# A decoder layer with product-key experts on one core: 160 instead of 144 gathered picks, dense products 352 columns wide

## Chip, core and metric

The kernel runs on one core of one Trainium2 chip. The metric is the time of one launch on the device in microseconds (us). Times of the kernel before are the median of three runs.

## What is computed

One layer for 512 tokens of width 2048, in float32. It has multi-head latent attention and a chunked spatial gating unit, an output projection, a PEER retrieval over 16,384 single-neuron experts, a gated per-layer embedding and a final norm. The change is about PEER alone:

```python
q = (a @ w_q).reshape(B, S, 8, 256)
s1, s2 = scores of the two halves of q against k1, k2      # 128 keys each, per head
...                                                        # top 16 of each, then top 16 of the 256 sums
experts = ...                                              # (token, head, 16): indices into 16,384 rows
gates = softmax(top)
h = einsum(u_exp[experts], a)                              # one dot product of 2048 per pick
out = einsum(gates * gelu(h), v_exp[experts])              # weighted sum of rows of v_exp
```

A token uses 8 x 16 = 128 of the 16,384 experts. `u_exp` and `v_exp` are 128 MB each.

## The kernel before

**Two ways to do PEER.** The tokens are split. The first `TD` = 368 tokens go the dense way: every expert is computed for every one of them. The weights of `u_exp` pass through as 128 chunks of 1 MB (128 experts each); a chunk gives a product of 128 experts by 368 tokens, which is scaled (`scale_chunk`, L1369), passed through gelu on ScalarE (L766) and stored to memory (`pre`). The gates of the dense tokens are scattered by GpSimd with indirect adds (`add_gates`, L518, 384 of them, one for each of three token tiles, 8 heads and 16 picks) into a matrix in memory that is zero but for the picks (`gates`, blanked by the fills of L488). Later each chunk of pre-activations and gates is loaded (L404, L405), multiplied on GpSimd (`apply_gates`, L545), split in a high and a low part (ScalarE L822, `weight_lo` L1475) and multiplied with `v_exp`, which passes as 16 groups of 8 slots of 1 MB. The result is added to the residual `hT` (`accumulate`, L1480).

The other 144 tokens go the sparse way: rows are gathered. A gather fetches one row of `uv_rows` (u and v side by side, 16 KB) for each of 128 partitions, 2 MB, by an indirect DMA that GpSimd issues (`gather`, L537). VectorE forms the dot products with the u half (`dot`, L1449), ScalarE makes gelu times gate of them (`weigh_pick`, L839 and L843), and VectorE adds the weighted v half to an accumulator (`add_row`, L1458, L1463). Two kinds of picks exist. *A picks* (`A_PICKS` = 128): the last 128 tokens, one token on each partition, one pick each. *B picks* (`B_PICKS` = 16): `BT` = 16 further tokens, each on 8 partitions (`SETS` = 8), one for each head, so 16 gathers cover their 128 picks. Their index tables are rearranged by small DMAs on ScalarE's queue (`bring_set`), their activations are spread by `spread_tokens`, and at the end a matmul with `sel` sums the partitions of a token.

**Matmuls.** Weights and activations are split in two float32r parts, and each product is three matmuls (`three`, L1637 to L1639: high x high, high x low, low x high). The high part of a weight tile is a copy by ScalarE (`hi`, L582), the low part a subtraction by VectorE (`lo`, L967), both for each MB of the stream. `wH` and `wL` have two buffers. The raw tiles have two, and four in most of the V stage (`raw_at`).

**Order.** Every engine's program is in order and written out by hand. In the head stage each of 8 heads takes two tiles of the query projection (512 columns) and four U chunks, with the top-k search on VectorE. Then come U chunks 32 to 127. From chunk 36 on the steps of the picks are spread over the slots: a pick has two steps, the dot and the add, and `u_step(c)` and `v_step(g, q)` say how many half steps are done before a slot. Picks 0 to 59 lie in the chunks up to 118, four more in the last eight chunks, and the rest, up to `PICKS` = 144, in the 118 V slots from the third to the end of group 14. The last group has none. A VectorE slot of V is: accumulate, first pick step, `lo`, other pick steps, accumulate, `weight_lo`. The row tiles: three buffers for the first picks, then two in turn (`ROW_AT`). A gather waits until the pick that used its buffer is added (`pick_done`). GpSimd does 164 scatter-adds (`ADDS_FIRST`), then gathers with four adds between them until the 384 are done, then `apply_gates` with the later gathers between. SyncE issues the raw loads, and in V between each two of them one chunk of pre-activations and gates (`load_late_chunk`), which waits for `act_wlo` of the chunk before the last.

Of the kernel before, what the change touches and what calls it, by code (L numbers as in the profile page):

```python
# [27 lines left out]
HEADS = 8  # L28
# [4 lines left out]
TOPK = 16  # L33
KEYS = 128
EPS = 1e-6
BT = 16
TA = T - P
TD = TA - BT
NTD = NT - 1
SETS = P // BT  # L40
PARTS = SETS // HEADS
A_PICKS = HEADS * TOPK
B_PICKS = TOPK // PARTS
PICKS = A_PICKS + B_PICKS
GROUP = 8
NGROUPS = KEYS // GROUP
# [105 lines left out]
def trunk_layer(nc, a, stream, out, gates_dram, pre_dram):  # L152
    F, R, U32, I32 = mybir.dt.float32, mybir.dt.float32r, mybir.dt.uint32, mybir.dt.int32
# [5 lines left out]
    KB = 1024  # L159

    def at(name, shape, dt, offset):
        return nc.alloc_sbuf_tensor_at(name, [P] + shape, dt, offset=base + offset)


    H0, A0, RING0, W0, M0, C0 = 0, 32 * KB, 96 * KB, 144 * KB, 176 * KB, 192 * KB
# [80 lines left out]
    ident = at("ident", [P], F, C0 + 12 * KB)  # L246
    iota = at("iota", [TOPK], F, C0 + 12 * KB + 512)
    idx_b = at("idx_b", [B_PICKS], U32, C0 + 12 * KB + 576)
    gates_b = at("gates_b", [B_PICKS], F, C0 + 12 * KB + 640)
    dots_b = at("dots_b", [B_PICKS], F, C0 + 12 * KB + 704)  # L250
    pick_wb = at("pick_wb", [B_PICKS], F, C0 + 12 * KB + 768)
    sel = at("sel", [BT], F, C0 + 12 * KB + 832)
    identR = at("identR", [P], R, C0 + 13 * KB)
    causalR = at("causalR", [P], R, C0 + 13 * KB + 512)
    dots = at("dots", [P], F, C0 + 13 * KB)
    pick_w = at("pick_w", [P], F, C0 + 13 * KB + 512)
    ones = at("ones", [P], F, C0 + 14 * KB)
    gains = at("gains", [NGAINS], F, C0 + 14 * KB + 512)
    smax = at("smax", [32], F, C0 + 14 * KB + 864)
# [10 lines left out]
    with ctx:  # L270
# [298 lines left out]
        def _(act):  # L569
# [136 lines left out]
            for n in range(ITEMS + 3):  # L706
# [16 lines left out]
                if n >= 5 and (n - 5) % NT == 3:  # L723
                    h = (n - 5) // NT
# [121 lines left out]

            def bring_set(i):

                h, r = divmod(i, PARTS)
                dst = slice(i * BT, (i + 1) * BT)  # L850
                src = slice(h * TOPK + r * B_PICKS, h * TOPK + (r + 1) * B_PICKS)
                act.dma_start(idx_b[dst, :], idx_e[at_b:P, src]).then_inc(b_loaded, 16)
                act.dma_start(gates_b[dst, :], gates_r[at_b:P, NTD - 1, src]).then_inc(b_loaded, 16)

            for c in range(ROUTE_U + 2, KEYS - GROUP):
                u_beat(c, c % 2, nu + c, 0)
                if c == ROUTE_U + 6:
                    act.wait_ge(routed, HEADS)
                if 0 <= c - ROUTE_U - 6 < SETS:
                    bring_set(c - ROUTE_U - 6)  # L860
                for o in range(u_step(c), u_step(c + 1)):
                    if o % 2 == 0:
                        weigh_pick(o // 2)
# [91 lines left out]
        def _(dve):  # L955
# [415 lines left out]
            def spread_tokens():  # L1371

                r4 = b_rep[:, :, :].rearrange("p k (r t) -> p k r t", t=BT)
                st.did(V.tensor_tensor(r4, hT[:, :, TD:TA].unsqueeze(2).to_broadcast([P, KD, SETS, BT]),
                                       gains[:, GAINS["ffn"]:GAINS["ffn"] + KD].unsqueeze(2).unsqueeze(3)
# [711 lines left out]
```

## Time and profile before

| | |
|---|---|
| median of 3 runs | 3095.76 us (3092.18 to 3096.97) |
| the profiled execution, its own time | 3098.32 us |
| its span, first to last instruction | 3096.6 us |
| mean granted TensorE clock | 0.994 |
| busy: TensorE, VectorE, ScalarE, GpSimd | 98%, 72%, 34%, 39% |
| memory traffic | 768.6 MB, mean 248 GB/s |

The page gives busy times by engine, the span in 40 slices of 77 us (busy tenths, granted clock, GB/s), the chain of work that ended last, and groups of instructions. A matmul's duration reaches from its start to the end of its pipeline and overlaps the next; the distance of two starts is what it takes of TensorE's time. The DMA share is the mean busy share of the core's 16 DMA engines; over short windows it can exceed 1.

### The profile page before, as it was taken

Reading aid. Unit: us, or ns where it says so; the run is one execution under the profiler, and the core shown is the slowest. Engines: PE = TensorE matmul, PEld = TensorE weight load, DVE = VectorE, ACT = ScalarE, POOL = GpSimd, SP = SyncE. Lnnn points to the kernel's source line nnn. Section 1 sums busy time; section 2 is a strip of 40 time slices with the busy share of each in tenths; the row PEclk is TensorE's granted clock in tenths of the full one; section 3 lists DMA queues with packets and bytes.
Section 4 is the critical chain, followed back from the end, with each engine's and each line's share of the span. In section 5 each row is a group of like instructions: output and inputs, shape, how many; then the busy total and the mean of one; then the engine's idle time right before and its main releaser. Section 6 shows DMA issues by size and latency. Waiting matters only on the chain.

```text
span 3096.6 us, 42534 instructions
## 1 busy us (share of the span) xinstructions
PE 3043.2 (98%) x16860; PEld 2854.9 (92%) x16860; DVE 2226.1 (72%) x2944; ACT 1061.3 (34%) x1328; POOL 1206.3 (39%) x702
## 2 busy tenths in 40 slices
PE   8999999999999999999999999999999999998998
PEld 6888668899999999999999999999999999998887
DVE  5465653478778777777777658888888888985545
ACT  5224442333332433333333333333333333333422
POOL 1010000018888788788887112332332333440000
PEclk9999999999999999999999999999999999999999
DMA  8472212245545599999999779899989989873222
GB/s 305 145 248 85 106 51 98 83 130 129 131 125 131 136 362 352 342 350 350 340 332 366 276 313 352 347 358 362 360 354 364 356 339 370 352 302 135 100 95 95
DMA packets 191488, 768.59 MB, mean 248 GB/s; under 512 B 68609, under 2 KB 121873, under 8 KB 129393
## 3 DMA queue, kind: packets, MB, share of 16 engines
q1 hardware_dynamic: 90768, 407.45, 35.9%
q0 software_dynamic: 81632, 335.12, 30.2%
q10 hardware_dynamic: 18944, 24.14, 2.3%
q8 instruction: 85, 1.39, 0.2%
q14 instruction: 59, 0.48, 0.0%
HBM read 714.00 MB, written 52.62 MB: 248 GB/s over the span
## 4 chain that ended last, share of the span: by engine, by line
PE 92%; DVE 3%; DMA 2%; issue 1%; ACT 1%; SPq 0%; POOL 0%; POOLq 0%; DVEq 0%; ACTq 0%
PE ps L1637 30%; PE ps L1638 30%; PE ps L1639 30%; DMA gate_in<-gates 1%; DVE wL L967 1%; DMA raw<-s_pu 1%; PE ps L1810 1%; PE ps L1829 1%; PE ps L1809 1%; PE ps L1872 0%; DMA raw<-s_v 0%; ACT wH L582 0%; DVE hT L1458 0%; DVE ssum L979 0%; PE ps L1819 0%
## 5 line engine op out<-in xcount | busy, mean ns | idle before, releaser
L1637 PE MATMUL ps<-aH,wH 128*128 128x368 f32 (+2 forms) x3088 | 1075.5, 348 | 6.5 <-DVE wL L967 4.4
L1638 PE MATMUL ps<-aL,wH 128*128 128x368 f32 (+2 forms) x3088 | 1071.6, 347 | 0.0
L1639 PE MATMUL ps<-aH,wL 128*128 128x368 f32 (+2 forms) x3088 | 1071.6, 347 | 0.0
L582 ACT ACTIVATE wH<-raw 128x2048 fp32r<-128x2048 f32 x333 | 637.7, 1915 | 1015.3 <-PE ps L1639 881.2
L967 DVE TENSOR_TENSOR wL<-raw,wH 128x2048 fp32r<-128x2048 f32 x333 | 786.2, 2361 | 195.3 <-ACT wH L582 194.4
L518 POOL DMA_INDIRECT gates<-gates_r,idx_d x384 | 745.9, 1942 | 370.5 <-DVE gates_r L1360 237.5
L1637 PE MATMUL ps<-actH,wH 128*128 128x368 f32 x2048 | 676.4, 330 | 12.5 <-DVE wL L967 10.3
L1638 PE MATMUL ps<-actL,wH 128*128 128x368 f32 x2048 | 675.7, 330 | 0.0
L1639 PE MATMUL ps<-actH,wL 128*128 128x368 f32 x2048 | 675.4, 330 | 0.0
L1637 PEld LDWEIGHTS ps<-aH,wH 128*128 128x128 f32 x3088 | 580.2, 188 | 46.4 <-DVE wL L967 5.5
L1638 PEld LDWEIGHTS ps<-aL,wH 128*128 128x128 f32 x3088 | 580.3, 188 | 38.7 <-issue 1.0
L1639 PEld LDWEIGHTS ps<-aH,wL 128*128 128x128 f32 x3088 | 580.2, 188 | 38.5
L1637 PEld LDWEIGHTS ps<-actH,wH 128*128 128x128 f32 x2048 | 386.4, 189 | 13.8 <-DVE wL L967 11.3
L1638 PEld LDWEIGHTS ps<-actL,wH 128*128 128x128 f32 x2048 | 386.4, 189 | 0.0
L1639 PEld LDWEIGHTS ps<-actH,wL 128*128 128x128 f32 x2048 | 386.4, 189 | 0.0
L545 POOL TENSOR_TENSOR pre_in<-pre_in,gate_in 128x368 f32<-128x368 f32 x128 | 181.4, 1417 | 434.1 <-DMA gate_in<-gates 431.8
L537 POOL DMA_INDIRECT rows<-uv_rows,idx_s x128 | 214.6, 1676 | 333.8 <-DVE hT L1458 295.9
L1449 DVE SCALAR_TENSOR_TENSOR rows<-rows,ps 128x2048 f32<-128x2048 f32 x128 | 291.6, 2278 | 16.3 <-DMA rows<-uv_rows,idx_s 15.8
L1458 DVE SCALAR_TENSOR_TENSOR hT<-rows,pick_w,hT 128x2048 f32<-128x2048 f32 x128 | 300.3, 2346 | 0.0
L1369 DVE TENSOR_TENSOR ut<-ps,rstd 128x368 f32<-128x368 f32 x128 | 69.1, 540 | 211.0 <-PE ps L1639 191.9
L1480 DVE TENSOR_TENSOR hT<-hT,ps 128x368 f32<-128x368 f32 x256 | 135.7, 531 | 93.5 <-PE ps L1639 93.5
L1475 DVE TENSOR_TENSOR actL<-pre_in,actH 128x368 fp32r<-128x368 f32 x128 | 85.6, 669 | 50.7 <-ACT actH L822 50.7
(258 smaller groups left out, 1890.5 us busy)
## 6 DMA issues: line engine op xcount, KB each, us to landing
raw<-s_pu SPq DMA_DIRECT2D x128, 1024.0 KB
raw<-s_pv SPq DMA_DIRECT2D x128, 1024.0 KB
gates<-zeros POOLq DMA_DIRECT2D x23, 1024.0 KB, 8.5
pre<-ut ACTq DMA_DIRECT2D x128, 184.0 KB
pre_in<-pre SPq DMA_DIRECT2D x128, 184.0 KB
gate_in<-gates SPq DMA_DIRECT2D x128, 184.0 KB
raw<-s_out SPq DMA_DIRECT2D x16, 1024.0 KB
raw<-s_pq SPq DMA_DIRECT2D x16, 1024.0 KB
```

Of the source, the lines that this page charges most:

```text
L518: pool.indirect_dma_start(out=gates_flat, out_offset=bass.IndirectOffsetOnAxis(ap=idx_d[0:m, t, c:c + 1], axis=0), in_=gates_r[0:m, t, c:c ...
L537: pool.indirect_dma_start(out=rows[ROW_AT[j]][:, :, :].rearrange("p a d -> p (a d)"), out_offset=None, in_=a["uv_rows"], in_offset=bass.In ...
L545: nc.gpsimd.tensor_tensor(pre_in[b][:, :], pre_in[b][:, :], gate_in[b][:, :], ALU.mult).then_inc(act_gated, 1)
L582: A(wH[parity][:, :], raw[at_n][:, :], ACT.Copy).then_inc(hi_ready, 1)
L967: V.tensor_tensor(wL[parity][:, :], src[:, :], wH[parity][:, :].bitcast(F), ALU.subtract).then_inc(lo_ready, 1)
L1449: V.scalar_tensor_tensor(r3, r3, 1.0, act_of, ALU.mult, ALU.mult, accum_out=d).then_inc(dot_done, 1)
L1458: V.scalar_tensor_tensor(hT[:, :, TA:T], v3, pick_w[:, j:j + 1], hT[:, :, TA:T], ALU.mult, ALU.add).then_inc(pick_done, 1)
L1475: V.tensor_tensor(actL[b][:, j, 0:TD], src[:, :], actH[b][:, j, 0:TD].bitcast(F), ALU.subtract).then_inc(act_wlo, 1)
L1480: V.tensor_tensor(h, h, ps[:, 4 + k % 4, 0:TD], ALU.add).then_inc(h_acc, 1)
L1637: mm(out, wh, xh, start=start, stop=False)
L1638: mm(out, wh, xl, start=False, stop=False)
L1639: return mm(out, wl, xh, start=False, stop=stop)
```

## The change

The split of the tokens moves by 16. `BT` becomes 32, so `TD` becomes 352 and every dense product, store, load, multiplication and accumulate has 352 columns. The b tokens are 32, each on 4 partitions (`SETS` = 4); a partition takes the picks of a pair of heads, 32 (`B_PICKS`), so the picks are 160. `v_step` spreads 96 instead of 80 of them over the same 118 V slots; `u_step` does not depend on their number. The gates' fills become 22. The small tables of the b picks are moved: `dots_b` and `pick_wb` are now views of the first columns of `dots` and `pick_w`, the tables of the A picks.

```diff
-BT = 16
+BT = 32
 TA = T - P
 TD = TA - BT
 NTD = NT - 1
 SETS = P // BT
-PARTS = SETS // HEADS
 A_PICKS = HEADS * TOPK
-B_PICKS = TOPK // PARTS
+B_PICKS = A_PICKS // SETS
 PICKS = A_PICKS + B_PICKS
...
-    gates_b = at("gates_b", [B_PICKS], F, C0 + 12 * KB + 640)
-    dots_b = at("dots_b", [B_PICKS], F, C0 + 12 * KB + 704)
-    pick_wb = at("pick_wb", [B_PICKS], F, C0 + 12 * KB + 768)
+    gates_b = at("gates_b", [B_PICKS], F, C0 + 12 * KB + 704)
...
+    dots_b, pick_wb = dots[:, 0:B_PICKS], pick_w[:, 0:B_PICKS]
...
-                h, r = divmod(i, PARTS)
                 dst = slice(i * BT, (i + 1) * BT)
-                src = slice(h * TOPK + r * B_PICKS, h * TOPK + (r + 1) * B_PICKS)
+                src = slice(i * B_PICKS, (i + 1) * B_PICKS)
```

## Rows read from the trace of the kernel before

**Rows 1.** The page: GB/s in the 40 slices of 77 us.
```profile
GB/s 305 145 248 85 106 51 98 83 130 129 131 125 131 136 362 352 342 350 350 340 332 366 276 313 352 347 358 362 360 354 364 356 339 370 352 302 135 100 95 95
```
**Rows 2.** The page: the chain that ended last, share of the span by line.
```profile
PE ps L1637 30%; PE ps L1638 30%; PE ps L1639 30%; DMA gate_in<-gates 1%; DVE wL L967 1%; DMA raw<-s_pu 1%; PE ps L1810 1%; PE ps L1829 1%; PE ps L1809 1%; PE ps L1872 0%; DMA raw<-s_v 0%; ACT wH L582 0%; DVE hT L1458 0%; DVE ssum L979 0%; PE ps L1819 0%
```
**Rows 3.** TensorE's waits, the longest in total: us, times, longest us.
```profile
PE ps L1637 <- DVE wL L967: 15.8, 7, 6.1
```
**Rows 4.** Stretches: length, busy us of PE, PEld, DVE, ACT, POOL; clock, DMA share, GB/s.
```profile
1100.00:1700.00 600.00, 600.00 (x3602) 600.00 (x3601) 451.55 (x316) 201.36 (x262) 482.87 (x268) 1.00 0.97 347
...
1762.00:1861.00 99.00, 95.46 (x572) 94.86 (x571) 62.48 (x52) 35.98 (x43) 14.78 (x15) 1.00 0.77 299
...
1900.00:2700.00 800.00, 800.00 (x4802) 800.00 (x4801) 697.37 (x604) 266.49 (x337) 268.37 (x168) 1.00 0.91 357
...
2770.00:2810.00 40.00, 30.27 (x166) 29.35 (x164) 21.67 (x18) 8.04 (x11) 3.89 (x4) 0.91 0.44 160
...
2064.00:2072.00 8.00, 8.00 (x50) 8.00 (x49) 6.56 (x8) 2.82 (x4) 1.66 (x2) 1.00 1.02 418
```
**Rows 5.** Timeline of TensorE: start us, duration us, neighbouring matmuls of 368 and of 512 columns.
```profile
860.15 0.33 PE L1639 MATMUL ps<-aH,wL 128*128 128x368 f32 x1
860.32 0.33 PE L1637 MATMUL ps<-aH,wH 128*128 128x368 f32 x1
...
2990.06 0.39 PE L1639 MATMUL ps<-aH,wL 128*128 128x512 f32 x1
2990.29 0.39 PE L1637 MATMUL ps<-aH,wH 128*128 128x512 f32 x1
```
**Rows 6.** Timeline of ScalarE in V: two weight copies, each released by TensorE.
```profile
2066.23 1.92 ACT L582 ACTIVATE wH<-raw 128x2048 fp32r<-128x2048 f32 x1 [5.68 <-PE ps L1639]
...
2074.23 1.92 ACT L582 ACTIVATE wH<-raw 128x2048 fp32r<-128x2048 f32 x1 [4.35 <-PE ps L1639]
```
**Rows 7.** Groups of VectorE by form: count, busy us, mean ns, idle before and releaser.
```profile
L967 DVE TENSOR_TENSOR wL<-raw,wH 128x2048 fp32r<-128x2048 f32 x333 | 786.2, 2361 | 195.3 <-ACT wH L582 194.4
L1458 DVE SCALAR_TENSOR_TENSOR hT<-rows,pick_w,hT 128x2048 f32<-128x2048 f32 x128 | 300.3, 2346 | 0.0
L1449 DVE SCALAR_TENSOR_TENSOR rows<-rows,ps 128x2048 f32<-128x2048 f32 x128 | 291.6, 2278 | 16.3 <-DMA rows<-uv_rows,idx_s 15.8 <-issue 0.2
L1480 DVE TENSOR_TENSOR hT<-hT,ps 128x368 f32<-128x368 f32 x256 | 135.7, 531 | 93.5 <-PE ps L1639 93.5
```
**Rows 8.** V, 1900 to 2700 us: two gathers, dots that waited for them, all such waits.
```profile
2160.17 0.96 POOL L537 DMA_INDIRECT rows<-uv_rows,idx_s  x1 [0.16 <-issue]
...
2549.97 2.85 POOL L537 DMA_INDIRECT rows<-uv_rows,idx_s  x1 [0.16 <-issue]
...
2171.29 2.29 DVE L1449 SCALAR_TENSOR_TENSOR rows<-rows,ps 128x2048 f32<-128x2048 f32 x1 [0.56 <-DMA rows<-uv_rows,idx_s]
...
2563.61 2.29 DVE L1449 SCALAR_TENSOR_TENSOR rows<-rows,ps 128x2048 f32<-128x2048 f32 x1 [0.90 <-DMA rows<-uv_rows,idx_s]
...
DVE rows L1449 <- DMA rows<-uv_rows,idx_s: 9.6, 11, 1.6
```
**Rows 9.** U: gathers, two of the dots, and the gathers' waits for a free buffer.
```profile
1077.96 1.00 POOL L537 DMA_INDIRECT rows<-uv_rows,idx_s  x1 [3.77 <-DVE ps L1435]
...
1089.97 1.00 POOL L537 DMA_INDIRECT rows<-uv_rows,idx_s  x1 [0.30 <-issue]
...
1614.60 1.36 POOL L537 DMA_INDIRECT rows<-uv_rows,idx_s  x1 [0.30 <-issue]
...
1684.70 1.00 POOL L537 DMA_INDIRECT rows<-uv_rows,idx_s  x1 [0.30 <-issue]
...
1090.54 2.27 DVE L1449 SCALAR_TENSOR_TENSOR rows<-rows,ps 128x2048 f32<-128x2048 f32 x1
...
1626.54 2.27 DVE L1449 SCALAR_TENSOR_TENSOR rows<-rows,ps 128x2048 f32<-128x2048 f32 x1
...
POOL rows L537 <- DVE hT L1458: 17.9, 11, 3.0
```

## The prediction

> **What bounds the kernel now.** I read the page first. TensorE is busy for 98% of the span (the table above), and the core's memory traffic jumps from about 130 to about 350 GB/s a third of the way in, where the row gathers begin [rows 1]. The chain that ended last is nine tenths TensorE, three lines with 30% each, the dense products [rows 2]. The list of TensorE's waits then shows how little it ever stands still: the largest entry is 15.8 us in 7 waits, for the low half of a weight tile [rows 3]. So a matmul that gets shorter is paid out in full, as long as all that feeds TensorE keeps up. The stretches [rows 4] say how near the feeders are to their own limits. In 600 us of the U stage TensorE never rests, VectorE is busy for 452 us (0.75), GpSimd for 483, and the DMA engines 0.97, moving 347 GB/s. In 800 us of the V stage TensorE never rests either, VectorE is busy for 697 us (0.87) and the DMA engines 0.91, moving 357 GB/s. That is the reader's main point: TensorE is the bound, but two or three others stand within a tenth behind it, and this change shortens TensorE's work and lengthens theirs.
>
> **The matmuls.** Neighbouring matmuls of 368 columns start 166 to 167 ns apart, those of 512 columns 227 ns [rows 5]. The difference, 60 ns for 144 columns, is 0.42 ns a column; so 352 columns should take 160 ns. A chunk of U (16 blocks times 3) or a slot of V (2 tiles times 8 times 3) has 48 of them: 8.00 us now, which is what two starts of the weight copy show [rows 6], and 7.68 us after. There are 256 such units: 256 x 0.32 = 82 us if TensorE stays the bound everywhere. The granted clock is 1.00 (the 2.4 GHz level) in all long dense stretches [rows 4].
>
> **The head stage, 32 chunks of U.** Up to 1046 us traffic is about 130 GB/s [rows 1] and no picks run. Nothing else is near its limit: 32 x 0.32 = **-10.2 us**.
>
> **U chunks 32 to 119, 88 of them, picks 0 to 59.** At best -28.2 us. The picks' number does not change here (60 over 82 chunks), their pace does: one in 10.93 us before, one in 10.49 after. Two things can hold this back. GpSimd: gather 2 starts at 1089.97 and gather 56 at 1684.70, 11.01 us each, of which it waited only 17.9 us in all for a free buffer [rows 9]; its own pace, with four scatter-adds between gathers, is (594.7 - 17.9) / 54 = 10.7 us, a little slower than 10.49. The lead of a gather over its dot product falls to 11.9 us at its tightest (1614.60 to 1626.54), about a landing time [rows 8, 9]. And the first gather: the 164 adds ahead of it do not get quicker, so it starts at best 3.8 us earlier (it had waited that long), while the chunks stand 10.2 us earlier; the 12.6 us between it and its dot (1077.96 to 1090.54) become about 6 [rows 9], and VectorE waits some 5 us once. The DMA engines: a chunk moves 1.05 MB of weights, 0.18 of stores and 0.73 x 2.10 of rows, 2.76 MB; at 7.68 us that is 360 GB/s, where 347 took a share of 0.97, so 358 a full one [rows 4]. I take 10 us as given back (between 0 and 20): **-18 us**.
>
> **The changeover, chunks 120 to 127 and the first V slots.** TensorE is busy only 95.5 of 99 us, VectorE 62.5 and the DMA engines 0.77 [rows 4]: nobody is full, so what is awaited there are loads and buffers in turn, not work. A faster TensorE waits longer: **0** (bounds -5 and +5). The same for the five slots at 2770 to 2810, busy 30.3 of 40 us at clock 0.91: **0**. The last eight V slots, without picks: **-2.6 us**.
>
> **V slots with picks, some 106 beside those.** Picks 64 to 159 instead of 64 to 143 go into the same 118 slots: 0.814 a slot instead of 0.678. TensorE alone would give 106 x -0.32 = -34 us. Against it stand three prices.
> - VectorE: a pick costs 2.28 + 2.35 = 4.63 us [rows 7]. At 0.136 more per slot that adds 0.63 us to the 6.97 us of now (697 us in 100 slots) [rows 4]; columns fewer give back some 0.06 (2.35 us for 2048 columns is 1.15 ns a column; three operations with 16 fewer). 7.54 us of 7.68: all but full, not over.
> - DMA: a slot moves 1.05 (weights) + 0.36 (gates and pre-activations) + 0.814 x 2.10 (rows) = 3.12 MB instead of 2.85. At 7.68 us that is 406 GB/s. The V row gives 357 GB/s at 0.91, so 392 at a full share: 7.95 us. One window of 8 us did show 418 GB/s [rows 4], so the edge is not hard.
> - Row tiles: two buffers in turn, so dot product, weight split and row add (2.3 + 2.4 + 2.35 = 7.0 us), then the gather, must fit into two picks, 2.46 slots. Gathers that VectorE waited for took 11.1 us (2160.17 to 2171.29) and 13.6 us (2549.97 to 2563.61) from GpSimd's start [rows 8]. With 0.2 us to start a gather that makes (7.2 + 11.1) / 2.46 = 7.4 us (no bound) and (7.2 + 13.6) / 2.46 = 8.46 us a slot.
>
> The prices meet in one in-order VectorE, whose lateness reaches the weight split and so TensorE. I take 8.10 us, above the DMA edge of 7.95 and below 8.46: 106 x 0.10 = **+11 us**.
>
> The Trainium skill, "DMA: Bandwidth & Descriptors", section "Where 436 GB/s comes from", puts the fabric's ceiling at 435 GB/s and says that transfers from HBM are bound at about 358 GB/s per core. By the first the slot would be 3.12 / 435 = 7.2 us, an estimate, and by the second 8.7 us. The window at 418 GB/s speaks for the first; the plateau of 339 to 370, 356 in the mean, in eleven slices of the V stage [rows 1] looks like the second.
>
> **Small edits.** 22 instead of 23 blank fills, and 8 instead of 16 small loads of indices and gates on ScalarE's queue: both lie behind TensorE's uninterrupted work of their stages, and without that cover they would be a gain, not a loss: 0. The sum of the b tokens is 512 instead of 256 wide; by the accumulate of 368 columns in 0.53 us [rows 7] that is some 0.3 us more on VectorE, in the last V slots, where it has room: 0. No wait is added for a chunk or a slot, but behind a late row on VectorE now stand the next weight split, the accumulates and the activation split, and SyncE's next loads wait for those.
>
> **Sum.** -10.2 - 18 + 0 - 2.6 + 11 = -20 us against the profiled execution's own 3098.3 us (span 3096.6): 3078. That execution stood 2.6 us above the median of 3095.8, so 3075.5 as a median. Differences of under 0.2% (6 us) can't be told from none here.
>
> **Rivals.**
> 1. *TensorE stays the bound* because the DMA engines reach 406 GB/s, as they did 418 for 8 us. V slots at 7.75: 106 x -0.25 = -26.5, U in full -28.2, with the rest -67: 3028. Against it: 0.91 x 3.12 / 2.85 x 8 / 7.68 = 1.04 of a full share. 0.16.
> 2. *The two row tiles decide* (slower). Place: the gather of pick j+2 behind the add of pick j. Price: 8.46 us a slot if every landing takes the 13.6 us of the longer one, 106 x 0.46 = +49, -31 elsewhere: +18, 3113. It decides once a landing takes over 2.46 x 8.00 - 7.2 = 12.5 us. For it: the longer landing is above that already, and landings should lengthen as the DMA engines fill. Against it: the other is below, and only 11 of some 68 dots (0.678 a slot) waited for a row at all, 9.6 us in sum [rows 8]. 0.19.
> 3. *The memory rate does not rise above its plateau*, say 360 GB/s: 3.12 / 360 = 8.67 us a slot, 106 x 0.67 = +71, with the rest +40: 3136. The 8 us window at 418 speaks against it. The figure of 358 GB/s per core in the Trainium skill ("DMA: Bandwidth & Descriptors", section "Where 436 GB/s comes from") would be this case. 0.08.
>
> **The forecast's own range**: slots from 7.95 (-5) to 8.25 us (+26), U between -28 and -8: 3047 to 3101; chance 0.57. The range 3032 to 3120 takes in rival 2 and half of rival 1, and leaves out rival 3 and the tails. Faster: nine tenths of the forecast and rival 1, 0.66; same 0.08; slower 0.26.
>
> **What would show it.** Matmul starts 160 ns apart; heads 1.28 us shorter; in the V stretches DMA share 0.97 or more near 385 GB/s, VectorE over 0.93 busy, TensorE waiting for the weight split for the first time in mid-stretch, some 0.4 us a slot; dots waiting for rows in most slots. Wrong: V stretches with TensorE still at 1.00 (rival 1), or a granted clock below 1.00 there after long waits, which no row prices for this stretch and which would push towards rival 2 or beyond.

## The result: 0.35% slower, and the profile after

Before: 3098.0 us, the median of twelve runs (3092.2 to 3105.2). After: 3108.3 us, the median of twelve runs on the same chip (3099.4 to 3125.2). The ratio is 1.0035, with a 95% interval of 1.0023 to 1.0046. The forecast was a gain of 20 us; the change costs 10.

Three lines of the changed kernel's page: the granted clock and the GB/s in the 40 slices (78 us each), and the chain that ended last, by line [rows 1, 2].

```profile
PEclk9999999999999999999999999999999999998999
GB/s 302 148 234 86 105 55 95 88 126 139 121 137 133 183 359 345 352 369 354 349 352 362 278 353 368 399 366 386 378 367 365 396 357 368 371 310 136 102 95 95
...
POOL gates L516 22%; PE ps L1634 10%; PE ps L1635 10%; PE ps L1636 10%; DMA rows<-uv_rows,idx_s 8%; DMA gate_in<-gates 6%; DMA rows<-uv_rows,idx_b 4%; DVE wL L964 4%; DVE hT L1455 3%; DVE rows L1446 3%; POOL rows L535 2%; DVE b_acc L1460 1%; DMA gates<-gates_r,idx_d 1%; DVE hT L1477 1%; POOL pre_in L543 1%
```

The chain was nine tenths TensorE before. Now a third of it is TensorE, and 12% is the landing of gathered rows, which was no part of it. (The 22% of L516 are the scatter-adds of the U stage. TensorE rests for only 2 of 600 us there, so the chain probably had two nearly equal ways back; the positions below show that this stage did get faster.)

The stretches: length, busy us of PE, PEld, DVE, ACT, POOL, then clock, DMA share and GB/s [rows 4].

```profile
1100.00:1700.00 600.00, 597.94 (x3710) 597.36 (x3709) 467.03 (x327) 206.09 (x270) 480.48 (x266) 1.00 1.00 357
...
1762.00:1861.00 99.00, 91.12 (x552) 89.67 (x551) 67.87 (x60) 34.18 (x41) 21.08 (x18) 0.98 0.87 343
...
1900.00:2700.00 800.00, 760.86 (x4620) 752.48 (x4619) 712.17 (x617) 258.75 (x349) 276.58 (x174) 0.98 0.95 374
...
2770.00:2810.00 40.00, 29.26 (x166) 28.09 (x164) 25.65 (x23) 8.29 (x12) 5.65 (x4) 0.91 0.56 212
```

In the 800 us of the V stage TensorE now stands still for 39 us. Neither of the two feeders that I had at their edge is there: VectorE is busy for 712 us (0.89) and the DMA share is 0.95. The waits of that stretch, for TensorE and for VectorE, name what is late:

```profile
PE ps L1634 <- DVE wL L964: 38.9, 25, 4.2
...
DVE rows L1446 <- DMA rows<-uv_rows,idx_s: 43.0, 28, 4.5
DVE actL L1472 <- ACT actH L820: 16.6, 30, 0.6
DVE hT L1477 <- PE ps L1636: 15.7, 18, 1.9
DVE rows L1446 <- DMA rows<-uv_rows,idx_b: 12.1, 11, 2.9
```

The kernel before, same stretch:

```profile
DVE hT L1480 <- PE ps L1639: 74.6, 55, 2.2
```

VectorE waits 55 us for gathered rows (10 before, [rows 8]) and little for TensorE (15.7 us; it was 74.6). All of TensorE's idle time comes from the weight split behind such a row. Here is one case from the timeline, VectorE's dot products (L1446), row adds (L1455), splits (L964), GpSimd's multiplication (L543) and gathers (L535), and the matmul that waited:

```profile
2261.03 2.34 DVE L1455 SCALAR_TENSOR_TENSOR hT<-rows,pick_w,hT 128x2048 f32<-128x2048 f32 x1
...
2264.16 2.22 POOL L543 TENSOR_TENSOR pre_in<-pre_in,gate_in 128x352 f32<-128x352 f32 x1 [7.34 <-DMA gate_in<-gates]
2265.50 2.28 DVE L1446 SCALAR_TENSOR_TENSOR rows<-rows,ps 128x2048 f32<-128x2048 f32 x1
2266.53 0.97 POOL L535 DMA_INDIRECT rows<-uv_rows,idx_s  x1
...
2271.91 2.28 DVE L964 TENSOR_TENSOR wL<-raw,wH 128x2048 fp32r<-128x2048 f32 x1
2272.26 2.78 POOL L535 DMA_INDIRECT rows<-uv_rows,idx_s  x1 [3.40 <-DVE hT L1455]
...
2278.64 2.29 DVE L1446 SCALAR_TENSOR_TENSOR rows<-rows,ps 128x2048 f32<-128x2048 f32 x1 [4.46 <-DMA rows<-uv_rows,idx_s]
2282.80 2.34 DVE L1455 SCALAR_TENSOR_TENSOR hT<-rows,pick_w,hT 128x2048 f32<-128x2048 f32 x1
2285.06 2.28 DVE L964 TENSOR_TENSOR wL<-raw,wH 128x2048 fp32r<-128x2048 f32 x1
2287.40 0.43 PE L1634 MATMUL ps<-actH,wH 128*128 128x352 f32 x1 [4.21 <-DVE wL L964]
```

The add that frees the row tile ends at 2263.37. GpSimd is held by a multiplication, which itself had waited for its gates, and starts the gather at 2266.53. The row is there 12.1 us later, at 2278.64. VectorE has stood for 4.46 us, and TensorE then for 4.21. The granted clock falls with it: it is 0.91 in the 10 us of this wait and 0.92 in the next 10.

```profile
2280.00:2290.00 10.00, 5.79 (x31) 5.50 (x31) 9.45 (x11) 4.87 (x6) 4.66 (x3) 0.91 0.66 242
2290.00:2300.00 10.00, 10.00 (x60) 10.00 (x59) 10.00 (x8) 2.81 (x4) 1.93 (x2) 0.92 1.03 424
2300.00:2310.00 10.00, 10.00 (x64) 10.00 (x63) 8.95 (x10) 3.49 (x7) 2.26 (x2) 1.00 1.01 407
```

**Where the time went, by position.** The table gives the start in us of the scaling of U chunks 31 and 127, of `weight_lo` of V slots 6, 110 and 119, and of the last two accumulates, in each profile. "A slot" is the distance of slots 6 and 110 over 104; "rows" is what dot products of the V stage waited for gathers. Each row is one execution. Kernels with the same U stage differ by up to 10 us at U 127, so a single difference means little under that size there, and under 5 us elsewhere. The variants are described in the next section.

| kernel | U 31 | U 127 | V 6 | V 110 | V 119 | last | a slot | rows |
|---|---|---|---|---|---|---|---|---|
| before | 1056.3 | 1830.2 | 1888.6 | 2720.3 | 2810.1 | 2881.3 | 8.00 | 10.5 |
| after | 1045.7 | 1798.4 | 1859.5 | 2726.0 | 2817.3 | 2889.0 | 8.33 | 63.6 |
| columns only | 1048.8 | 1808.5 | 1865.0 | 2668.3 | 2755.8 | 2825.5 | 7.72 | 25.2 |
| picks only | 1057.0 | 1831.3 | 1892.5 | 2761.8 | 2854.7 | 2924.9 | 8.36 | 63.4 |
| after, u half only | 1044.1 | 1801.1 | 1856.3 | 2663.8 | 2750.8 | 2820.6 | 7.76 | 0 |
| after, split rows | 1048.6 | 1809.0 | 1870.0 | 2695.4 | 2785.2 | 2855.0 | 7.94 | 0 |
| after, third tile | 1044.7 | 1804.3 | 1865.3 | 2695.6 | 2767.8 | 2837.7 | 7.98 | 0 |
| after, ring of two | 1047.3 | 1803.9 | 1859.8 | 2723.3 | 2801.4 | 2872.2 | 8.30 | 69.8 |
| before, ring of two | 1060.1 | 1834.3 | 1888.7 | 2720.4 | 2794.7 | 2866.6 | 8.00 | 7.7 |
| before, third tile | 1060.6 | 1834.3 | 1893.3 | 2725.2 | 2798.7 | 2873.0 | 8.00 | 0 |
| before, split rows | 1055.4 | 1829.5 | 1888.8 | 2720.8 | 2810.0 | 2881.1 | 8.00 | 0 |
| picks only, split rows | 1057.6 | 1831.7 | 1893.9 | 2750.6 | 2841.2 | 2911.5 | 8.24 | 0 |
| picks only, third tile | 1055.5 | 1830.2 | 1890.8 | 2727.9 | 2802.3 | 2874.6 | 8.05 | 0 |
| after, split rows, 160 adds | 1045.8 | 1798.6 | 1859.7 | 2685.6 | 2775.5 | 2845.4 | 7.94 | 0 |

After is 31.8 us ahead at the end of U and 29.1 at V slot 6. At slot 110 it is 5.7 behind. The 104 slots between lost 34.8 us.

### The profile page after: what moved, and what is told of

It reads as the page before. It is cut to its first block, busy times and chain, and to the rows that moved or that the text cites. A ratio compares the mean times of both kernels' runs of the same rounds, so it can differ in the third digit from the quotient of the medians.

```text
span 3104.3 us, 42637 instructions
## 1 busy us (share of the span) xinstructions
PE 2996.5 (97%) x16860; PEld 2795.3 (90%) x16860; DVE 2279.2 (73%) x2992; ACT 1062.5 (34%) x1360; POOL 1222.0 (39%) x717
## 4 chain that ended last, share of the span: by engine, by line
PE 32%; POOL 24%; DMA 19%; DVE 13%; issue 8%; ACT 2%; SPq 0%; POOLq 0%; ACTq 0%; DVEq 0%
POOL gates L516 22%; PE ps L1634 10%; PE ps L1635 10%; PE ps L1636 10%; DMA rows<-uv_rows,idx_s 8%; DMA gate_in<-gates 6%; DMA rows<-uv_rows,idx_b 4%; DVE wL L964 4%; DVE hT L1455 3%; DVE rows L1446 3%; POOL rows L535 2%; DVE b_acc L1460 1%; DMA gates<-gates_r,idx_d 1%; DVE hT L1477 1%; POOL pre_in L543 1%
## 5 line engine op out<-in xcount | busy, mean ns | idle before, releaser
L1634 PE MATMUL ps<-aH,wH 128*128 128x352 f32 (+2 forms) x3088 | 1063.9, 345 | 8.8 <-DVE wL L964 6.7
L1635 PE MATMUL ps<-aL,wH 128*128 128x352 f32 (+2 forms) x3088 | 1062.1, 344 | 0.0
L1636 PE MATMUL ps<-aH,wL 128*128 128x352 f32 (+2 forms) x3088 | 1059.6, 343 | 0.0
L964 DVE TENSOR_TENSOR wL<-raw,wH 128x2048 fp32r<-128x2048 f32 x333 | 780.5, 2344 | 196.0 <-ACT wH L580 193.4
L516 POOL DMA_INDIRECT gates<-gates_r,idx_d x384 | 758.9, 1976 | 370.3 <-DVE gates_r L1357 235.8
L1634 PE MATMUL ps<-actH,wH 128*128 128x352 f32 x2048 | 675.1, 330 | 63.3 <-DVE wL L964 60.3
L1635 PE MATMUL ps<-actL,wH 128*128 128x352 f32 x2048 | 670.2, 327 | 0.0
L1636 PE MATMUL ps<-actH,wL 128*128 128x352 f32 x2048 | 669.8, 327 | 0.0
L1446 DVE SCALAR_TENSOR_TENSOR rows<-rows,ps 128x2048 f32<-128x2048 f32 x128 | 292.1, 2282 | 70.3 <-DMA rows<-uv_rows,idx_s 69.2
L535 POOL DMA_INDIRECT rows<-uv_rows,idx_s x128 | 193.5, 1512 | 347.8 <-DVE hT L1455 312.3
L543 POOL TENSOR_TENSOR pre_in<-pre_in,gate_in 128x352 f32<-128x352 f32 x128 | 174.5, 1364 | 353.7 <-DMA gate_in<-gates 352.9
L1455 DVE SCALAR_TENSOR_TENSOR hT<-rows,pick_w,hT 128x2048 f32<-128x2048 f32 x128 | 300.6, 2349 | 0.4 <-ACT pick_w L841 0.3
L837 ACT ACTIVATE dots<-dots 128x1 f32<-128x1 f32 x160 | 32.5, 203 | 581.9 <-DVE rows L1446 540.4
L1366 DVE TENSOR_TENSOR ut<-ps,rstd 128x352 f32<-128x352 f32 x128 | 66.9, 523 | 165.7 <-PE ps L1636 117.6
L1477 DVE TENSOR_TENSOR hT<-hT,ps 128x352 f32<-128x352 f32 x256 | 130.8, 512 | 25.9 <-PE ps L1636 25.9
```

The lines of the kernel that those rows point to most:

```text
L516: pool.indirect_dma_start(out=gates_flat, out_offset=bass.IndirectOffsetOnAxis(ap=idx_d[0:m, t, c:c + 1], axis=0), in_=gates_r[0:m, t, c:c ...
L535: pool.indirect_dma_start(out=rows[ROW_AT[j]][:, :, :].rearrange("p a d -> p (a d)"), out_offset=None, in_=a["uv_rows"], in_offset=bass.In ...
L543: nc.gpsimd.tensor_tensor(pre_in[b][:, :], pre_in[b][:, :], gate_in[b][:, :], ALU.mult).then_inc(act_gated, 1)
L964: V.tensor_tensor(wL[parity][:, :], src[:, :], wH[parity][:, :].bitcast(F), ALU.subtract).then_inc(lo_ready, 1)
L1366: V.tensor_tensor(ut[b][:, :], ps[:, 6 + b, 0:TD], rstd[:, 0:TD], ALU.mult).then_inc(chunk_scaled, 1)
L1446: V.scalar_tensor_tensor(r3, r3, 1.0, act_of, ALU.mult, ALU.mult, accum_out=d).then_inc(dot_done, 1)
```

## The experiments

The main theory: the cycle of one of two whole row tiles (dot, split, add, gather, landing) is longer than two picks now last, and everything behind the late row is late. The rivals: VectorE is simply full; the memory rate is at its limit; and later, that the order of the raw loads holds the stage back. Each ratio is against the kernel before, run beside the variant on the same chip. The chips differ from group to group (the kernel before took 3095.4 to 3099.7 us on them), so medians of different groups compare to within some 4 us.

**Split rows.** One row tile is released in halves: the u half can be refilled once the dot has read it, the v half once the add has. The bytes, the picks and the matmuls stay.

```diff
-                        if o % 2 == 1 and o // 2 + 2 < PICKS:
-                            gather(o // 2 + 2)
+                        if o // 2 + 2 < PICKS:
+                            gather_half(o // 2 + 2, o % 2 == 1)
...
+                if ROW_USED[j] >= 0:
+                    pool.wait_ge(pick_done if out else dot_done, ROW_USED[j] + 1)
...
+                    out=rows[ROW_AT[j]][:, 1 if out else 0, :], out_offset=None, in_=a["v_rows" if out else "u_rows"],
```

> The changed kernel, but for picks 64 to 159 a row is fetched by two gathers, the u half and the v half, each into its half of the same two row tiles. The u half may be refilled after the dot product, the v half after the add. The same bytes; 96 more gather instructions on GpSimd. Theory A (the two row tiles decide: dot, weight split, add and a landing of 11 to 14 us must fit into two picks): each half has only 2.3 us of use in its cycle, so the V slot falls from 8.33 us to the DMA edge, 3.12 MB at a full share (374 GB/s at 0.95, so 394 GB/s), 7.92 us; 104 x 0.41 = 43 us less than the changed kernel, some 3065 us, and the waits of dots for rows shrink from 64 us to under 15. Theory B (the DMA engines' rate decides, about 374 GB/s over the V stage whatever the buffers do): slot 8.3 us, 3108 us as the changed kernel, GB/s unchanged. Theory C (VectorE's work decides): slot unchanged or longer by the slower instructions beside more gathers.

Measured: 3065.8 us (3061.3 to 3072.5), ratio 0.989 (0.9872 to 0.9908). The V stretch:

```profile
1900.00:2700.00 800.00, 782.72 (x4842) 776.49 (x4842) 772.41 (x651) 273.43 (x366) 471.61 (x266) 1.00 0.99 394
```

No dot of this stretch waits for a row any more, and the traffic flows at 394 GB/s instead of 374. GpSimd pays with 195 us more (one more indirect DMA a pick), which nothing waits for. The same picks and bytes pass faster, at a higher memory rate and with VectorE busier. So neither of these two had made the changed kernel slow.

**Columns only, picks only.** The change has two parts. The first kernel keeps the 352 columns and takes 144 picks, so half of the experts of the 32 b tokens are left out; the second keeps 368 columns and takes 160, 16 of them experts that the b tokens should not have.

```diff
-B_PICKS = A_PICKS // SETS
+B_PICKS = A_PICKS // SETS // 2
```
```diff
-B_PICKS = TOPK // PARTS
+B_PICKS = 2 * TOPK // PARTS
```

> The changed kernel with 144 picks: 352 columns in all dense products, but the 32 b tokens get only the first of their two heads on each partition (16 of 32 b picks are left out), so the output of those tokens lacks half of their experts. Shows what the narrower products give without more picks. Every theory: U as in the changed kernel (32 us less than before), V demand 2.83 MB a slot, 369 GB/s at 7.68 us, a share of 0.94, and two picks last 22.7 us against 7.2 + 13.6. Theory A: V slots 7.7 to 7.8 us, total 3098 - 32 - 104 x 0.25 = about 3040 us. Theory B (rate capped near 374): 7.68 us is 369, the same 3035 to 3045. If slots stay at 8.0, something not counted (GpSimd or the chunk loads) holds V.

> The kernel before with 160 picks: 368 columns and 16 b tokens as before, but each partition takes 32 b picks instead of 16, the additional 16 being those of the next head (for the last head those of the one before), so the b tokens sum too many experts. Shows what 16 more picks cost without narrower products. Theory A: slot max(8.0, (7.2 + landing) / 2.46) with landings of 11 to 14 us, 8.4 us or more: 104 x 0.4 = 42 us over before, 3140 us. Theory B: 3.14 MB at 374 GB/s is 8.4 us as well, and at 394 GB/s 8.0 us, 3098 to 3140. Theory C (VectorE, 7.6 us of work in an 8.0 us slot): no change, 3098 us.

Measured: columns 3040.9 us (3037.7 to 3045.1), ratio 0.9814 (0.9795 to 0.9834); picks 3141.0 us (3138.6 to 3145.6), ratio 1.0139 (1.0119 to 1.0158). The parts make 0.9814 x 1.0139 = 0.9950 together, the change 1.0035: they do more harm together than one by one, by 0.8% (26 us). The V stretches of both:

```profile
1900.00:2700.00 800.00, 798.82 (x4969) 797.30 (x4969) 702.06 (x624) 272.89 (x346) 266.20 (x173) 1.00 0.94 366
```
```profile
1900.00:2700.00 800.00, 775.95 (x4591) 769.92 (x4590) 716.49 (x617) 257.59 (x348) 266.00 (x174) 0.99 0.96 376
```

In the V slots the columns alone pay nearly in full (7.72 us, where TensorE needs 7.68), with a pick period of 11.4 us. The picks alone raise the slot to 8.36 us, what it is after (8.33), although each slot has 0.32 us more of matmuls: at 160 picks and two tiles the slot goes by the tiles and not by TensorE.

**The u half only.** The gathers of the V stage fetch 1 MB instead of 2, into the same tile with the same releases, and the add reads the u half. VectorE's work is unchanged.

```diff
+                half = ROW_AT[j] >= 3
...
-                    out=rows[ROW_AT[j]][:, :, :].rearrange("p a d -> p (a d)"), out_offset=None, in_=a["uv_rows"],
+                    out=rows[ROW_AT[j]][:, 0, :] if half else rows[ROW_AT[j]][:, :, :].rearrange("p a d -> p (a d)"), out_offset=None,
+                    in_=a["u_rows"] if half else a["uv_rows"],
```

> The changed kernel, but the gathers of picks 64 to 159 fetch only the u half of a row (1 MB instead of 2 for 128 partitions), and the add uses that half: VectorE's, GpSimd's and TensorE's instructions are the same, the gathered bytes of V are halved (v rows are left out of those picks). Theories A and B both: landings of 6 to 8 us and 2.27 MB a slot, 295 GB/s, so V slots reach TensorE's 7.68 us, 3098 - 32 - 104 x 0.32 = about 3033 us. Theory C (VectorE's 7.5 us of work, in order): slots of 8.0 us or more, 3065 us or more.

Measured: 3041.6 us, ratio 0.9817 (0.9792 to 0.9842).

```profile
1900.00:2700.00 800.00, 797.60 (x4948) 794.37 (x4947) 772.21 (x664) 275.02 (x371) 289.23 (x187) 1.00 0.81 292
```

VectorE is busy for 772 of 800 us (0.97), TensorE rests 2.4 us and a slot takes 7.76 us: a VectorE as full as that costs at most 0.08 us a slot. With shorter landings the two tiles are enough. This alone can't tell tiles from memory rate, since both landing and traffic fell; the split rows and the third tile do.

**Controls with split rows.** The split in the kernel before, in the kernel with 160 picks and 368 columns, and the split kernel with 160 scatter-adds ahead of the first gather instead of 164 (its first dot had waited 9.9 us).

> The kernel before (368 columns, 144 picks) with the split gathers of e1_split_rows. Theory A (row tiles decide only where 160 picks meet 7.68 us): here TensorE's 8.00 us was the bound and the tiles were just fast enough, so nothing is gained: 3093 to 3099 us, slot 8.00; dots no longer wait for rows. If the split were a gain by itself (fewer late weight splits, a clock that never falls), it would be over 6 us faster.

> e3_picks_only (368 columns, 160 picks, some experts of the b tokens summed twice over) with the split gathers. e3 cost 44.6 us over before. Theory A: the slot is the larger of TensorE's 8.00 us and the DMA edge, 3.13 MB at 394 GB/s, 7.95 us; so nearly all 44.6 us vanish, 3096 to 3108 us. Theory B (16 more picks cost DMA rate whatever the tiles do) or C (VectorE): 3125 us or more.

> e1_split_rows with 160 instead of 164 scatter-adds ahead of the first gather (one more gather later has four behind it). In e1 the first dot waited 9.9 us for its row (gather at 1083.2, dot at 1091.7), in the changed kernel 1.4 us. GpSimd's four adds are 7.4 us: the first gather starts that much earlier, but not before a_tok, which was ready at 1069.7. Expected 5 to 7 us less than e1: 3059 to 3061 us. If only GpSimd's total work counts in U, no change: 3066 us.

Measured: 3098.1 us, ratio 1.0003 (0.9992 to 1.0014); 3122.6 us (3119.0 to 3128.7), ratio 1.0071 (1.0052 to 1.009); 3065.4 us (3062.9 to 3070.1), ratio 0.9895 (0.9877 to 0.9914). The first is the control that was wanted: where rows are not late, the split gives nothing. The second is a miss: 18.5 us better than without the split, but some 15 to 27 us above what I expected, with slots of 8.24 us and no dot waiting. The third is a null in the medians, where I had expected 5 us or more. Its profile says otherwise: the first dot waited 1.5 us instead of 9.9, and the way from U 31 to U 127 took 752.8 us instead of 760.4. But that execution was the fastest of its kernel and the other the slowest of its own, so the two profiles don't overrule the medians, and the point stays open. The first dots of the split kernel and of the changed kernel:

```profile
1091.68 2.29 DVE L1462 SCALAR_TENSOR_TENSOR rows<-rows,ps 128x2048 f32<-128x2048 f32 x1 [9.92 <-DMA rows<-uv_rows,idx_s]
...
1080.35 2.29 DVE L1446 SCALAR_TENSOR_TENSOR rows<-rows,ps 128x2048 f32<-128x2048 f32 x1 [1.43 <-DMA rows<-uv_rows,idx_s]
```

**A third row tile.** Three whole tiles instead of two. The room comes from the raw ring, which stays at two buffers in V; SyncE then loads one chunk and one value in turn.

```diff
-    _at = _j % 3 if _j < U_PICKS - LATE else 2 if _j < U_PICKS else 3 + _j % 2
+    _at = _j % 3 if _j < U_PICKS - LATE else 2 if _j < U_PICKS else 3 + _j % 3
...
-    v = n - S0["pv"]
-    return (v - 2) % 4 if 4 <= v < KEYS - GROUP else n % 2
+    return n % 2
...
-            for v in range(2, KEYS - GROUP):
+            for v in range(KEYS - GROUP):
                 load_late_chunk(v)
-                load_value(v + 4)
+                load_value(v + 2)
...
-                        if o % 2 == 1 and o // 2 + 2 < PICKS:
-                            gather(o // 2 + 2)
+                        if o % 2 == 1 and o // 2 + 3 < PICKS:
+                            gather(o // 2 + 3)
```

> The changed kernel with whole-row gathers, but three row tiles in turn in V instead of two, gathers issued three picks ahead; the 16 KB for the third are taken from the raw ring, which has two tiles in V instead of four, with SyncE's loads reordered to chunk v, value v+2. Theory A: with three tiles a landing may take 3 x 2.46 / 2 slots = 28.3 - 8.0 = 20 us before it matters, so rows are never waited for; slot 7.95 us (DMA edge) if two raw tiles are enough, 3066 us. With raw loads of about 10 us (as the 10.4 us of the changeover) against some 9 us of slack, weight copies may wait for raw: then up to 8.2 us a slot and 3090 us, with ScalarE's L580-copy waiting for DMA raw instead of dots for rows. Theory B: 8.3 us a slot, 3108 us.

Measured: **3053.1 us** (3046.1 to 3057.0), ratio 0.9845 (0.9822 to 0.9868), the fastest version that computes the whole layer.

```profile
1900.00:2700.00 800.00, 780.86 (x4812) 771.36 (x4811) 762.02 (x645) 270.99 (x362) 293.50 (x182) 1.00 0.99 391
...
DVE actL L1466 <- ACT actH L814: 23.7, 38, 0.9
DVE wL L958 <- ACT wH L574: 14.1, 14, 2.2
```

No wait for rows is left, and VectorE (0.95) and the DMA engines (0.99) both stand near their edge: this is close to the state that I had forecast for the change itself, at 7.98 us a slot. The time is 13 us below the 3066 that I had expected. Slots 110 to 119 took 72.3 us instead of the 89.8 with split rows (91.4 after), so the kernel had two changes in it.

**The ring alone, and all combinations.** The ring of two and its load order without the third tile, in both kernels; the third tile with 160 picks and 368 columns; and the third tile in the kernel before.

> The kernel before (368 columns, 144 picks, two whole row tiles) with the raw ring and the load order of e8_third_tile: two raw tiles all through V, SyncE issues chunk v, then value v+2. In the kernel before, SyncE has a gap of 24 us in its raw loads (2751.2 to 2775.2) where the ring goes from four tiles to two, and TensorE idles 10 us behind it. Theory A takes the 12 us that e8 is faster than e1 for this gap alone (from slot 110 to 119 it took 72 us, e1 90): expected 10 to 17 us less than before, 3080 to 3087 us, with slots of 8.00 us elsewhere. If two raw tiles are too few at 8.00 us, slots grow and it is slower than before.

> The changed kernel with that ring and load order, but still two whole row tiles in V. Theory A (the row tiles): V slots from 6 to 110 stay at 8.3 us, only the end is 10 to 17 us shorter: 3091 to 3098 us, 40 us over e8. If the order of SyncE's loads was what the row tiles seemed to be (theory D: chunks come earlier when they don't queue behind a load four slots ahead), slots fall to 8.0 us and the time to 3055 us.

> e3_picks_only (368 columns, 160 picks, some experts of the b tokens summed twice) with ring, order and third row tile of e8. e6 (split gathers) left 25 us of e3's 45: slots of 8.24 us although no dot waited, TensorE waiting 1.4 us for a weight split every 42 or 90 us. If that rest is the unevenness of VectorE's in-order program (two slots in a row with two pick steps take 9.8 us each), it stays here too: slots of 8.1 to 8.2 us, and with the 10 to 17 us of the end 3098 to 3112 us. If it was the slower VectorE instructions beside 96 more gather instructions, slots are 8.0 us: 3085 us.

> The kernel before (144 picks, 368 columns) with a ring of two raw tiles, the load order of one chunk and one value in turn, and three whole row tiles in the V stage. It closes the table of picks against row tiles. Theory: at 144 picks two row tiles are no bound (the pick period is 11.8 us, and a late row cost the kernel with the ring of two and two tiles 7.7 us in all), so a third tile gives nothing: 3078 to 3084, the 3081.9 of that kernel, slot 8.00 us. Rival: a third tile helps any kernel (fewer late rows, or the gathers spread over time): under 3075, and then the 27 us between 3053 with 160 picks and 352 columns and 3082 are not all the change's.

| median us (ratio, 95%) | two row tiles, ring of four | two row tiles, ring of two | three row tiles, ring of two |
|---|---|---|---|
| 144 picks, 368 columns | 3098.0 | 3081.9 (0.9918 to 0.9962) | 3085.8 (0.9939 to 0.9973) |
| 160 picks, 368 columns | 3141.0 (1.0119 to 1.0158) | | 3094.6 (0.998 to 1.0001) |
| 160 picks, 352 columns | 3108.3 (1.0023 to 1.0046) | 3089.9 (0.9959 to 0.9991) | 3053.1 (0.9822 to 0.9868) |

Three things stand in it. The ring of two with its load order is worth 16 to 18 us by the medians in either kernel with two row tiles, most of it between slots 110 and 119 (15.5 us of the kernel before, 13.3 of the changed one). The window at slots 110 to 114 of the kernel before with the ring of two, against 30.27 busy us in [rows 4], is

```profile
2770.00:2810.00 40.00, 40.00 (x248) 39.98 (x246) 30.90 (x25) 13.73 (x16) 8.87 (x4) 1.00 0.66 237
```

The third tile is worth nothing at 144 picks (+4 us, intervals that overlap) and 37 us at 160 picks and 352 columns. And the change itself, from the first line to the last, costs 10 us with two tiles (8 with the ring of two) and gains 33 with three. The two V stretches side by side, with the ring of two in both (kernel after with two tiles, then kernel before with three):

```profile
1900.00:2700.00 800.00, 759.70 (x4627) 750.13 (x4626) 714.13 (x620) 259.08 (x349) 269.37 (x176) 0.99 0.95 376
```
```profile
1900.00:2700.00 800.00, 800.00 (x4802) 800.00 (x4801) 702.74 (x605) 266.70 (x336) 273.53 (x168) 1.00 0.90 357
```

The middle row bears on the miss above. With 160 picks and 368 columns the third tile gives slots of 8.05 us, nearly the 8.00 of TensorE, and the split rows only 8.24 (third tile, then split rows):

```profile
1900.00:2700.00 800.00, 797.70 (x4779) 795.89 (x4778) 760.57 (x640) 270.90 (x362) 290.80 (x181) 1.00 0.99 389
```
```profile
1900.00:2700.00 800.00, 783.44 (x4677) 778.59 (x4676) 750.82 (x625) 261.54 (x352) 442.26 (x256) 1.00 0.97 381
```

So most of what held the split kernel was not an unevenness of 160 picks as such. The two kernels differ in the split, which has one more gather a pick, and in the raw ring; which step costs 0.2 us a slot is not shown. My expectations had left 3098 to 3112 us or 3085 for the kernel with the third tile, and its 3094.6 lies between. The other three came within 2 us of theirs.

**The cycle itself.** Mean us over picks 70 to 139, in three parts that make two pick periods (three with the third tile), whatever holds the kernel:

| kernel | dot start to add end | to the gather's start | gather to its dot | of those that waited | pick period | covers |
|---|---|---|---|---|---|---|
| before | 8.24 | 1.07 | 14.29 | 12.82 (11 of 70) | 11.82 | 2 |
| after | 7.19 | 0.82 | 12.45 | 11.81 (36 of 70) | 10.20 | 2 |
| columns only | 7.91 | 1.59 | 13.31 | 11.21 (26 of 70) | 11.43 | 2 |
| after, ring of two | 7.17 | 0.93 | 12.25 | 11.67 (36 of 70) | 10.15 | 2 |
| after, third tile | 7.65 | | 20.72 | none | 9.78 | 3 |

A pick period at 7.68 us a slot would be 9.44 us, and two of them 18.9. The cycle with its landing is 7.19 + 0.82 + 11.81 = 19.8. That is 8.06 us a slot if the program asked for each row in the moment it lands. The rows of the other 34 picks were not waited for, and the time from a gather to its dot has a mean of 12.45 us over all 70. With it the three parts make 20.46 / 2.46 = 8.32, the measured slot, but that is bookkeeping: the same sum gives 8.00 before. The cycle accounts for 8.06 us of the 8.33; the other 0.27 is tile time lost between a row's landing and its dot, which a program that asks at fixed places of the slot can lose; how it comes to 0.27 is not shown. What shows that the tiles decide is the split rows and the third tile.

**What lengthens a landing.** In the timeline above one gather keeps GpSimd for 0.97 us and the next for 2.78. The short one starts beside a dot product, the long one beside VectorE's weight split (L964). That is the rule in this stage: from 1900 to 2700 us, 35 of the 39 long gathers of the changed kernel overlap a weight split, and none of the 38 short ones does (34 of 34, and none of 33, before). The row then comes later by nearly as much: over picks 66 to 159, waited rows of short gathers came after 10.9 us (21 of them) and those of long ones after 12.5 (27). A gather that starts the moment an add ends often meets the weight split, which is next on VectorE. No run moved the split, so the price of this for the whole kernel is open.

## Why the prediction was wrong

- **Heads, -10.2 us.** -10.6 at chunk 31. Right. Two weight copies in the U stage start 7.73 us apart, near the 7.68 of the forecast, and matmuls of 352 columns 0.16 us apart, as said:

```profile
1410.99 1.92 ACT L580 ACTIVATE wH<-raw 128x2048 fp32r<-128x2048 f32 x1 [5.43 <-PE ps L1636]
1418.72 1.92 ACT L580 ACTIVATE wH<-raw 128x2048 fp32r<-128x2048 f32 x1 [4.48 <-issue]
...
2099.89 0.32 PE L1635 MATMUL ps<-actL,wH 128*128 128x352 f32 x1
2100.05 0.32 PE L1636 MATMUL ps<-actH,wL 128*128 128x352 f32 x1
```

- **U chunks 32 to 119, -18 us.** At chunk 127 the kernel is 31.8 us ahead, 21.2 more than at 31; the forecast had 18. The DMA share from 1100 to 1700 us is 1.00 at 357 GB/s, the price of 358 that I read off [rows 4]. Right within 3 us, but this profile flatters: its first dot waited only 1.43 us. In the five other profiles with this U stage and as many adds ahead of the first gather that dot waited 9.9 to 10.6 us, where I had said some 5, and the gain from 31 to 127 was 13.5 to 17.3 us. That is still in the range of 8 to 28 that I gave.
- **Changeover, five slots, last slots: 0, 0, -2.6 us.** +2.7 between chunk 127 and slot 6, and +2.0 from slot 110 to the last accumulate. Within 5 us together, the end slightly off.
- **V slots with picks, +11 us. This is the step that failed.** It measured +34.8 over 104 of them, 8.33 us a slot in place of the 8.10 that I took: 24 of the 28 us by which the profile missed the forecast. Of its three prices, VectorE (7.54 of 7.68) is hardly a bound even at 0.97 busy (7.76 us a slot), by the kernel with the u half only. The DMA edge of 7.95 fits the slots without late rows (7.94 split, 7.98 with three tiles). The third price, the row tiles, decided. I had worked it out at 7.4 to 8.46 and then took a value just above the DMA edge, as if the causes were averaged, where the slowest one holds the slot by itself. The landings were not longer than I had them: waited ones took 11.81 us, between my 11.1 and 13.6, and (7.2 + 0.2 + 11.8) / 2.46 is only 7.80. What I had wrong in the cycle is GpSimd's queue, 0.82 us instead of 0.2 (8.06 with it), and what I left out is the time in which a landed row lies unused, 0.27 us a slot more. The two landings of [rows 8] also hid something: the one of 11.1 us kept GpSimd for 0.96 us and the one of 13.6 for 2.85, the two kinds described above.
- **The clock.** I had named it as what would push the case towards rival 2, unpriced. In the 800 us TensorE is busy for 761 us; the 96 slots need 96 x 7.68 = 737. Of the 23 us between, some 14 are the lower granted clock after waits (the mean over the 800 us is 0.983), and the rest lies mostly in the starts after each of 25 waits and the ends of the matmuls before them. Where the row decides anyway the slower matmuls may only fill what would have been idle; no run shows that apart.
- **Rival 2** (two tiles decide, 8.46 a slot, 3113) had the mechanism and the sign: 3108 and 8.33. Its condition, "over 12.5 us of landing", was off, because it was set against 8.00 us a slot: against 7.68 it is 2.46 x 7.68 - 7.2 = 11.7 us, just what the waited landings took. That was in reach from the rows. That its 8.46 came near 8.33 is in part luck: it took every landing at 13.6 us, and they took 11.8, with the queue and the unused time in place of the rest.
- **The range.** Its lower end, 3047, adds up to 3050 from its own terms (3095.8 - 10.2 - 28 - 5 - 2.6); the measured 3108 lies above it all the same.
- **Rival 1** (TensorE stays the bound) falls at TensorE's 39 us of idle. **Rival 3** (a plateau of 360 GB/s) falls at 394 GB/s over 800 us. The Trainium skill, "DMA: Bandwidth & Descriptors", section "Where 436 GB/s comes from", lets HBM transfers end at about 358 GB/s; these runs disagree, with 394. The Trainium skill, "Perfetto Trace Analysis", section "Roofline", says that a core that is alone can pull more than that share, up to about 435 GB/s; 394 is below it, and the runs agree.

## What to carry to other kernels

When a change shortens the beat, take each buffer that is refilled, and add up its whole cycle (uses, the work between them, the queue of the engine that issues, the landing) against buffers times the new beat. The busy shares do not show it, because nobody in that cycle is full. If the sum comes close, expect some loss on top: here it gave 8.06 us against 7.68, and 8.33 were measured. Do the sum at the beat that you hope for, not at the one of now. If it does not fit, release parts of the buffer earlier or add one, before judging the change: the same edit was worth +10 us with two tiles and -33 with three.

## What was not expected of the hardware

- One core held 394 GB/s at a DMA share of 0.99 over 800 us, where the plateau of the kernel before (357) had looked like a limit. In the V stage it was demand, not a limit. In the U stage the share is 1.00 at the same 357 GB/s; its traffic has the scatter-adds and the stores in it, and what lowers the rate of a full share there was not tried.
- Landings of 2 MB of gathered rows did not get longer as the share rose from 0.91 to 0.95: 12.8 us before and 11.8 after, of those that were waited for (11 and 36). The selections differ, but by kind of gather it is the same: short ones 11.3 and 10.9 us, long ones 13.5 and 12.5.
- A gather keeps GpSimd for 0.97 us, or for 2.8 where VectorE's weight split runs beside it, and then its row lands 1.6 us later (10.9 and 12.5 us, of waited rows).
- A ring of four raw tiles, which ends eight slots before the stage, costs both kernels 13 to 16 us there, though the deeper ring was meant to hold more in flight. TensorE idled 10 of 40 us at that place; with a ring of two throughout, and its order of loads, it did not idle in the kernel before and 4 us in the changed one. Ring and order were changed together.
- The runs of the changed kernel spread over 26 us, those of the kernel before over 13. The first dot, which waits 1.4 us in one profile and 10 in another, may be a part of it.
